# Expert-weighted sum in four 64x64 matmul quadrants, two picks at a time, expert stage unrolled

## What is computed

```python
def block(h_t):                                   # h_t: 128 tokens x 1024
    q = jnp.einsum('td,dq->tq', h_t, w_query).reshape(T, PEER_HEADS, 2, PEER_HALF)
    s1 = jnp.einsum('thc,hkc->thk', q[:, :, 0], sub_keys_1)
    s2 = jnp.einsum('thc,hkc->thk', q[:, :, 1], sub_keys_2)
    ...                                           # top 16 of s1 and of s2, top 16 of their sums
    gates = jax.nn.softmax(top_s.astype(jnp.float32), axis=-1).reshape(T, PEER_HEADS * PEER_TOPK)
    u = expert_u[experts]
    act = jax.nn.gelu(jnp.einsum('td,tkd->tk', h_t, u).astype(jnp.float32), approximate=False)
    vv = expert_v[experts]
    return jnp.einsum('tk,tkd->td', (gates * act).astype(h_t.dtype), vv)
```

## Time and profile before

| | us |
|---|---|
| median of 3 runs | 3447.39 (3445.55 to 3451.28) |
| the profiled execution, time | 3441.94 |
| its span, first to last instruction | 3440.1 |
| PE busy | 2892.8 (84% of the span) |
| DVE busy | 2138.9 (62%) |
| POOL busy | 1396.5 (41%) |
| ACT busy | 1342.9 (39%) |
| moved by the indirect DMA | 1073.81 of 1122.28 MB |

### The profile page before, as it was taken

The page is one execution under the profiler, slowest core; times in us unless marked ns, Lnnn a source line. Parts: engine busy times, 40 slices in busy tenths (PEclk is TensorE's granted clock), DMA queues, the critical chain, the costliest instruction groups (busy, mean ns, idle before and its releaser), DMA issues.

```text
span 3440.1 us, 38782 instructions
## 1 busy us (share of the span) xinstructions
PE 2892.8 (84%) x8340; PEld 1429.7 (42%) x8340; DVE 2138.9 (62%) x4949; ACT 1342.9 (39%) x3773; POOL 1396.5 (41%) x1224
## 2 busy tenths in 40 slices
PE   8999677777889888888888888888888888888887
PEld 5443566644444333433343343334333433333332
DVE  1276444436666667666766666666667666766664
ACT  3043122124444444444444444444444444444443
POOL 0000222104444454455445544554455445554554
PEclk9999899989999999999999999999999999999999
DMA  3001000039999999999999999999999999999998
GB/s 126 31 34 61 1 1 0 0 122 408 420 421 406 401 422 421 402 393 422 422 379 418 422 398 395 422 422 402 396 422 422 395 393 422 422 420 396 422 421 351
DMA packets 164924, 1122.28 MB, mean 326 GB/s; under 512 B 18112, under 2 KB 23744, under 8 KB 33472
## 3 DMA queue, kind: packets, MB, share of 16 engines
q0 software_dynamic: 147456, 1073.81, 75.6%
q1 hardware_dynamic: 17344, 47.23, 3.7%
HBM read 1112.58 MB, written 8.39 MB: 326 GB/s over the span
## 4 chain that ended last, share of the span: by engine, by line
PE 31%; DMA 23%; issue 11%; ACT 6%; POOL 3%; DVE 3%; ACTq 0%; POOLq 0%; DVEq 0%
PE bank L1324 23%; DMA ring_mem<-in_experts,work 23%; PE bank L1308 5%; POOL ring_mem L978 3%; PE bank L1299 3%; ACT work L1073 3%; ACT work L1068 1%; ACT work L1065 1%; ACT L1065 1%; ACT L1037 1%; DVE ring_mem L1234 0%; DVE work L1234 0%; DVE work L1144 0%; PE bank L813 0%; PE bank L1289 0%
## 5 line engine op out<-in xcount | busy, mean ns | idle before, releaser
L1324 PE MATMUL bank<-ring_mem,work 128*128 128x512 f32 x4096 | 1952.9, 622 | 373.0 <-ACT work L1073 305.6
L978 POOL DMA_INDIRECT ring_mem<-in_experts,work x1024 | 1283.9, 1254 | 1330.5 <-PE bank L1324 1119.5
L1234 DVE CUSTOM_DVE_ANT_0 ring_mem<-ring_mem,work 128x1024 f32<-128x1024 f32 x1024 | 1251.4, 1222 | 560.8 <-DMA ring_mem<-in_experts,work 555.3
L1324 PEld LDWEIGHTS bank<-ring_mem,work 128*128 128x128 f32 x4096 | 765.3, 196 | 1515.3 <-ACT work L1073 752.7
L1065 ACT ACTIVATE work<-work 128x1 f32<-128x1 f32 x1024 | 206.2, 201 | 1118.2 <-DVE work L1234 1064.0
L1073 ACT ACTIVATE work<-kept,work 128x128 f32<-128x128 f32 x1024 | 411.2, 402 | 182.6 <-ACT work L1068 130.6
L1068 ACT ACTIVATE work<-work 128x1 f32<-128x1 f32 x1024 | 301.5, 294 | 172.1 <-ACT work L1065 109.9
L1308 PE MATMUL bank<-late,work 128*128 (+1 forms) x1024 | 236.7, 385 | 22.1 <-DVE work L1197 11.2
L1308 PEld LDWEIGHTS bank<-late,work 128*128 128x128 f32 x1024 | 197.1, 193 | 75.7 <-issue 51.3
L355 PE MATMUL bank<-ring_mem,late 128*128 128x512 f32 x512 | 221.9, 592 | 1.1 <-PEq L189 1.1
L1144 DVE MAX8 work<-bank 128x8 f32<-128x128 f32 x128 | 38.2, 299 | 267.6 <-PE bank L1308 267.3
(11 more groups left out here) (195 smaller groups left out, 1910.7 us busy)
## 6 DMA issues: line engine op xcount, KB each, us to landing
ring_mem<-in_experts,work POOLq DMA_INDIRECT x1024
late<-in_wc SPq DMA_DIRECT2D x16, 512.0 KB, 3.5
work<-in_w_query SPq DMA_DIRECT2D x10, 512.0 KB
x_all<-in_w_out SPq DMA_DIRECT2D x1, 4096.0 KB, 12.7
work<-in_x SPq DMA_DIRECT2D x8, 512.0 KB
out<-work SPq DMA_DIRECT2D x8, 512.0 KB
work<-mixed_tiles SPq DMA_DIRECT2D x7, 512.0 KB
work<-in_w_query SPq DMA_DIRECT2D x6, 576.0 KB, 4.9
```

What stands on the lines that cost most here:

```text
L978: G.indirect_dma_start(ring[k % RING], None, a["experts"], bass.IndirectOffsetOnAxis(ap=pick_now[:, k:k + 1], axis=0)).then_inc(got[k % RI ...
L1234: V.tensor_tensor_reduce(out=row, in0=row, in1=hf_now, scale=1.0, scalar=0.0, op0=ALU.mult, op1=ALU.add, accum_out=dots[:, k:k + 1]).then_ ...
L1324: m = PE.matmul(bank[6 + half], diag[k % RING], ring[k % RING][:, DM + half * HALF:DM + (half + 1) * HALF], start=(at(j, START) and k == 0 ...
```

## The change

1. The weighted sum takes two picks at a time. `diag` is now 128x64: the low 64 partitions hold the 64x64 diagonal of tokens 0 to 63, the high 64 that of tokens 64 to 127. Each pick, each half of the columns, is two matmuls of 64x64 weights. The four matmuls of a pair and a half go from low or high partitions to low or high partitions of the output: the even pick to its own partitions, the odd pick crosswise. The sums lie in four banks, `low_sum = bank[4:6]` and `high_sum = bank[6:8]`. PE waits for the odd pick's `diag`, and `used` goes up by two at the end of the pair.
2. At a tile's end ACT copies the crosswise sums into `out_tile` on the right partitions (`cross`, four 64x512 copies), before the new tile's first gelu. `take_sum` is then one 128x1024 addition and four 64x512 additions, where it was two of 128x512.
3. The projection moves to `bank[0:2]`, and that of tile 1 from ahead of tile 0 into tile 0, between heads 4 and 5. SP's load for tile 2's projection moves behind the loads of the queries.
4. All loops of the expert stage are written out, and the extra `sem_inc` and register instructions go.

```diff
-        diag = [cut(P) for _ in range(RING)]
+        diag = [cut(CHUNK) for _ in range(RING)]
...
+        low_sum, high_sum = bank[4:6], bank[6:8]
+        low, high = slice(0, CHUNK), slice(CHUNK, P)
...
-                with pool.Fori(0, TILES) as t:
-                    pool.sem_inc(pool_steps, 1)
-                    with pool.Fori(0, PHEADS) as j:
+                for t in range(TILES):
+                    for j in range(PHEADS):
...
-
-                sp.wait_ge(mixed_out, 2)
-                load_mixed(2)
                 load_queries(2 * HEADS_FIRST + 1)
...
+
+                sp.wait_ge(mixed_out, 2)
+                load_mixed(2)
...
+                def cross(t):
+
+                    act.wait_ge(X["used"], t * PICKS + (USED0 + PICKS))
+                    act.wait_ge(X["out_stored"], t * 16)
+                    for half in range(2):
+                        cols = slice(half * HALF, (half + 1) * HALF)
+                        A.activation(out_tile[low, cols], low_sum[half][high], ACT.Copy)
+                        m = A.activation(out_tile[high, cols], high_sum[half][low], ACT.Copy)
+                    m.then_inc(X["crossed"], 1)
...
-                            A.activation(diag[k % RING], ident, ACT.Copy, scale=weights[:, k:k + 1]).then_inc(X["diag_made"], 1)
+                            A.activation(diag[k % RING], pair_ident, ACT.Copy, scale=weights[:, k:k + 1]).then_inc(X["diag_made"], 1)
...
                     dve.wait_ge(X["used"], t * PICKS + (USED0 + PICKS))
+                    dve.wait_ge(X["crossed"], t + 1)
+                    vc.link(V.tensor_tensor(h_now, out_tile, h_now, ALU.add))
                     for half in range(2):
-                        h = h_now[:, half * HALF:(half + 1) * HALF]
-                        m = V.tensor_tensor(h, bank[6 + half], h, ALU.add)
+                        cols = slice(half * HALF, (half + 1) * HALF)
+                        V.tensor_tensor(h_now[low, cols], low_sum[half][low], h_now[low, cols], ALU.add)
+                        m = V.tensor_tensor(h_now[high, cols], high_sum[half][high], h_now[high, cols], ALU.add)
                     m.then_inc(X["summed"], 1)
...
-                    for k in range(TOPK):
+                    for k in range(1, TOPK, 2):
                         pe.wait_ge(X["diag_made"], t * PICKS + j * TOPK + (k + 1))
+                        opens, ends_sum = at(j, START) and k == 1, at(j, END) and k == TOPK - 1
                         for half in range(2):
-                            m = PE.matmul(bank[6 + half], diag[k % RING], ring[k % RING][:, DM + half * HALF:DM + (half + 1) * HALF],
-                                          start=(at(j, START) and k == 0), stop=(at(j, END) and k == TOPK - 1))
-                        m.then_inc(X["used"], 1)
+                            for odd in range(2):
+                                n = (k - 1 + odd) % RING
+                                row = ring[n][:, DM + half * HALF:DM + (half + 1) * HALF]
+                                PE.matmul(low_sum[half][high if odd else low], diag[n][low], row[low], start=opens, stop=ends_sum)
+                                m = PE.matmul(high_sum[half][low if odd else high], diag[n][high], row[high], start=opens, stop=ends_sum)
+                                if half == 1:
+                                    m.then_inc(X["used"], 1)
...
+                    if first:
+
+                        pe.wait_ge(M["w_score_kept"], 2 * PHEADS)
+                        project(1, 0)
+                        project(1, 1)
                     step(t, TURN, first, after, TURN + AHEAD)
...
                 head(0, 0)
-                project(1, 0)
-                project(1, 1)
                 head(1, 1)
```

More of the change, by code:

```diff
@@ L947, in makes_weights @@
         def makes_weights(first, j):
-            return first and (at(j, START) or not isinstance(j, int))
+            return first and j < TURN
         def at(j, head):
-            return isinstance(j, int) and j == head
+            return j == head
         with nc.Block() as block:
@@ L1011, in _ @@
                     load_queries(n)
-                with sp.Fori(0, TILES - 3) as t:
+                sp.wait_ge(mixed_out, 2)
+                load_mixed(2)
+                for t in range(TILES - 3):
                     sp.wait_ge(mixed_out, t + 3)
@@ L1058, in step @@
                 def step(t, j, first, last, jn):
+                    if at(j, START) and not first:
+                        cross(t - 1)
                     act.wait_ge(X["gates_scaled"], t * PHEADS + j + 1)
-                    act.sem_inc(scalar_steps, 1)
                     for m in range(GROUPS):
@@ L1089, in tile @@
                     step(t, START, first, last, 1)
-                    with act.Fori(1, TURN) as j:
+                    for j in range(1, TURN):
                         step(t, j, first, last, j + 1)
@@ L1100, in _ @@
                 tile(0, first=True)
-                with act.Fori(1, TILES - 1) as t:
+                for t in range(1, TILES - 1):
                     tile(t)
                 tile(TILES - 1, last=True)
+                cross(TILES - 1)
                 final_sum(TILES - 1)
@@ L1256, in tile @@
                     step(t, START, first, last, AHEAD, 1)
-                    V.sem_inc(vector_steps, 1)
-                    with vc.loop(1, TURN, PICK_LINKS + 1) as j:
+                    for j in range(1, TURN):
                         step(t, j, first, last, j + AHEAD, j + 1)
@@ L1275, in _ @@
                 tile(0, first=True)
-                with vc.loop(1, TILES - 1, PHEADS * (PICK_LINKS + 1) + 3) as t:
+                for t in range(1, TILES - 1):
                     tile(t)
@@ L1298, in project @@
                     for d in range(DB):
-                        m = PE.matmul(bank[3 + half], mixed[:, d * P:(d + 1) * P],
+                        m = PE.matmul(bank[half], mixed[:, d * P:(d + 1) * P],
                                       w_out[:, d * DM + half * HALF:d * DM + (half + 1) * HALF], start=(d == 0), stop=(d == DB - 1))
@@ L1313, in step @@
                     if first:
-                        pe.wait_ge(M["w_score_kept"], 2 * PHEADS if isinstance(j, int) and j > 0 else j * 2 + (2 * AHEAD + 2))
+                        pe.wait_ge(M["w_score_kept"], min(2 * PHEADS, j * 2 + (2 * AHEAD + 2)))
                     if jp is not None:
@@ L1332, in step @@
                             weight_product(some_queries, some_keys, bank[0:2])
-                        if k == GROUP - 1 and after == 2 and isinstance(j, int) and j > TURN:
+                        if k == GROUP - 1 and after == 2 and j > TURN:
                             project(t + 2, j - TURN - 1)
@@ L1339, in tile @@
                     step(t, START, first, after, AHEAD)
-                    with pe.Fori(1, TURN) as j:
+                    for j in range(1, TURN):
                         step(t, j, first, after, j + AHEAD)
+                    if first:
+                        pe.wait_ge(M["w_score_kept"], 2 * PHEADS)
+                        project(1, 0)
+                        project(1, 1)
                     step(t, TURN, first, after, TURN + AHEAD)
@@ L1350, in _ @@
                 pe.wait_ge(X["hf_kept"], 1)
-                pe.sem_inc(tensor_steps, 1)
                 head(0, 0)
-                project(1, 0)
-                project(1, 1)
                 head(1, 1)
                 tile(0, first=True)
-                with pe.Fori(1, TILES - 2) as t:
+                for t in range(1, TILES - 2):
                     tile(t)
```

43 lines of the change are left out of this document (13 added, 30 removed).

## The result

| | us |
|---|---|
| median of the changed kernel, 5 runs | 3506.42 (3496.5 to 3512.05) |
| the kernel before beside it | 3447.39 |
| ratio | 1.0164, 95% interval 1.0144 to 1.0184 |
| the profiled execution: time, span | 3512.05, 3510.3 |

The account below looks back on a forecast made before the run. Transfers were taken as the bound, with at most 68 us left for a faster PE. Terms 8 + 24 + 14 + 9 + 12 + 7 = 74 us over 3441.9 gave 3516, plus 5.5 for the median 3521; range 3445 to 3580.

Parts of the forecast that it names:

- The pair: Weighted sum of two picks: four quadrants work at once, 1.8 us at full clock and 3.4 at half.
- second rival: In the pair, two records in a row block the queue, so PE gains nothing; +99 us, 3546; chance 0.25.
- The clock: PE's low activity puts the pair before a head at half clock: 1.6 us late, scores 1.0 us longer.
- ordinary changes of head (heads 1 to 5): At 40 changes of head, fetch between 0.8 us inside and outside its limit: 0 to 32 us, taken as 8.
- changes of tile: At 7 changes, PE restarts 3.5 us later in five, 5.2 in two; two slots at once help 0.5: 24 us.
- head 6: Projection at head 6 in 6 tiles: late scores and the pair behind it add 2.4 us each, 14 us.
- head 7: At head 7 in 6 tiles: 1.2 us of reserve against about 2.7 of delay, 9 us.
- moved projection: Before head 5 of tile 0: 14 us of projection on PE, less 1.8 of remaining reserve, costs 12 us.
- end: Behind the last pick nothing covers copies 2.4, additions 2.6 and half-clock pair 1.6: 7 us.
- The loops: Written-out loops of the expert stage save 1.7 us of PE's wait, only at the 5 tile changes inside the loop.
- The reserve: At a change of head, pick 8's fetch may start 6.4 us later, by 1753.7, before its dot is late.
- The crossing: At a tile's end ACT's copies (2.4 us) hide under dots; `take_sum` grows from 1.27 to 3.9 us.

## Why the prediction was right, and where not

The forecast was 3521 with a range of 3445 to 3580; the median is 3506.4. For the profiled execution the sum gave 3516, and it took 3512.05. The 5.5 us that I added for the median had the wrong sign: this time the profiled execution lay 5.6 above its median.

**The bound** held: 422 GB/s undisturbed, 401 over the stage, and a PE that is busy for 550 us less brought nothing.

**The pair** held. The spacing that was to tell the cases apart shows 16 records in 1.7 us at full clock and 3.4 at half; one pick had taken 1.71. That is the forecast, and it rules out the second rival: the two records of one matmul do not hold up the matmuls of the other quadrants. The Trainium skill, "TensorE: Matmul & The Clock Gate", Part 3, says that matmuls start and end strictly in program order. In this trace the first records of four matmuls start in the order of the list, all within 0.02 us, and the rule cost nothing.

**The clock** held as a mechanism, and its reverse was shown: 38 us come back with idle work just ahead of the change of head, and 2 with the same work six picks (15 us) earlier. The sizes were too large. I took 1.6 us for the last pair and 1.0 for the scores; they cost 1.1 and 0.2 on average over the 28 changes, for I had the pair before a head always at half clock, and it was so in 20 of them.

**The steps of the sum,** from the table of heads (profiled executions, after less before):

| us | predicted | measured |
|---|---|---|
| ordinary changes of head (heads 1 to 5) | 8 | 26.3 in tiles 1 to 7 |
| changes of tile | 24 | 12.5 |
| head 6 | 14 | 0.4 |
| head 7 | 9 | 5.0 |
| moved projection | 12 | 15.6 at head 5, 21.7 for all of tile 0 |
| end | 7 | 5.1 |
| all | 74 | 70 |

The total is nearer than its terms. Two were mis-sized, in opposite directions, and that they cancel is luck.

*The loops.* I gave written-out loops 1.7 us at five changes of tile, 8.5 in all, from the one change outside the loop. They were worth 17, with 11.4 of the table at head 6, where I had not counted them. Against the version with written-out loops the changes of tile cost 24.2 and head 6 11.8, which are the 24 and 14 of the sum, though the 24 had 8.5 of the loops in it already.

*The reserve.* The step "inside the limit of 1753.7, so at ordinary changes of head the pairing costs nothing" failed. The run with whole matmuls in pairs sits on that limit by my count and loses over 1 us at each change of head. The changed kernel shows it more sharply. Counted from the last dot of a head, the limit is 1753.7 - 1736.9 = 16.8 us, and I had the fetch at 16.0 to 17.6. It left earlier, at 13.0 to 16.0 us, inside the limit in all 28 changes, and 20 of them still lost 1.2 us on average (the table under the clock). So I had the delay too large and its price too small. One of the 20, with the last dot at 2022.89: the fetch of pick 8 and its dot, then 8 us from that fetch on, and the same stretch of a head whose fetch left at 14.4 us:

```profile
2038.86 1.26 POOL L975 DMA_INDIRECT ring_mem<-in_experts,work  x1 [7.64 <-PE bank L1325]
...
2046.64 1.23 DVE L1232 CUSTOM_DVE_ANT_0 ring_mem<-ring_mem,work 128x1024 f32<-128x1024 f32 x1 [2.33 <-DMA ring_mem<-in_experts,work]
...
2038.89:2046.89 8.00, 5.00 (x44) 1.18 (x36) 5.44 (x18) 5.73 (x18) 6.48 (x6) 1.00 0.92 334
1917.38:1925.38 8.00, 3.73 (x32) 1.03 (x32) 5.27 (x16) 4.32 (x13) 4.81 (x5) 1.00 1.01 422
```

From fetch to dot it is 7.78 us here, and 6.3 to 8.4 in the 20 changes (7.1 on average), where I had taken 5.56 from an empty queue. Over the 8 us behind the fetch the rate is 334 GB/s and not 422; in the first 2 of them it is 373 already, while the landing of pick 7 is still to come. So both assumptions of the reserve fail: the full rate up to the last landing, and the 5.56. By these traces the ring bore a fetch at 14.7 us behind the last dot and not at 15.7. With the 10.4 of before (1747.32 - 1736.9), the reserve was between 4.3 and 5.3 us and not 6.4. Why the transfers slacken so early was not tested.

*The crossing* was 2.6 us at each of 7 tiles and 5 at the end, 23 us; it measured 25 at a high clock and 29 at a low one. The wait for `take_sum`, 8.7 us predicted, was 8.76; with the loops written out alone it was 6.0, so loops and additions were sized rightly there. That the copies hide at a change of tile and show at the end held in the trace of after, where DVE stands still behind the last of them:

```profile
3496.45 0.59 ACT L1042 ACTIVATE work<-bank 64x512 f32<-64x512 f32 x1 [2.09 <-PE bank L1325]
...
3498.96 1.23 DVE L1206 TENSOR_TENSOR work<-work 128x1024 f32<-128x1024 f32 x1 [5.54 <-ACT work L1043]
```

*Fetching code* was bounded by 0 to 6 us and taken as 0. The queue q8 carries 1.44 MB where it was 0.44, and the version with only the loops written out loses 2.2 to 3.3 us over 7 tiles at each of heads 3 to 5, where before nothing is lost. That is some 8 us in all; that code is the cause was not tested.

From before to after by medians of the experiments, each against its neighbour: loops -17, moved projection +8, two picks at a time at a good clock +9 (idle matmuls included), crossing and additions +25, low clock +36; together +61 for the 59 to 62 measured, since before came to 3444.5 in the later comparisons. Each step is the difference of two neighbouring versions, so that they add up is no proof of any of them.

## What to carry to other kernels

Halving the work of an engine that only looks busy bought nothing here, where another resource sets the pace, and it cost twice: through what the new form adds on the path of a hand-over (here five additions), and through the clock of the engine that now idles. Read a stage's bound from its rate (GB/s against an undisturbed stretch), find the few places where that rate breaks, and shorten the chain there: a second pair of banks for the sum took away a wait of 8 us that no faster matmul could reach. Judge the clock at the place that others wait for, and not by its mean.

## What the runs showed of the hardware

- 38 us were gained by giving TensorE idle work right before the change of head (3468.07 against 3506.42), and 2 by the same amount six picks earlier (3504.26), both at a mean granted clock of 0.87 in the stage.
- In the changed kernel the last pair before heads 2 to 5 ran at a granted clock of 0.50 to 0.56 in 20 of 28 cases and at 1.00 in 8. The 20 heads lost 24.7 us together and the 8 lost 1.9.
- With eight slots and 2.49 us per landing, a fetch of pick 8 that left 15.7 to 16.0 us behind the last dot of the old head took 6.3 to 8.4 us to its dot; from a ring that had run dry it took 5.3 to 5.9 at the seven changes of tile.
- fp32 matmuls of 64x64 in four quadrants, two records each, start within 0.02 us of each other; 16 records of 512 columns take 1.7 us, against 3.4 for the same products as whole matmuls of two picks.
- A 64x512 addition on DVE with one operand in a bank takes 0.68 us, and the two of 128x512 in the earlier trace rows take 1.27: half the partitions save nothing, so the sum of two halves costs double.
